# Latent attention, first head of a layer: the last memory head's transposes and values, and the pair's projection, placed inside the first gate chunk

## What is computed

```python
for l in range(DEPTH_2):                       # 2 layers
    h = rmsnorm_2(x, pre_norm_g[l])
    z = h @ w_in[l]
    q_lat, kv_lat, k_pe, gb, gc, xin, q_mem, gate = split_cols(z)
    q = (rmsnorm_2(q_lat, q_norm_g[l]) @ w_uq[l])       # 8 heads, 128 + 64 rotated columns
    kv = (rmsnorm_2(kv_lat, kv_norm_g[l]) @ w_ukv[l])   # 8 heads, 128 of key, 128 of value
    a_out = mla_attention(q, k, v)                      # the latent attention
    c_out = short_gated_conv(gb, gc, xin, conv_w[l])
    m_out = memory_attention(q_mem, mem_n, w_mk[l], w_mv[l])   # 4 heads over 256 memory tokens
    y = jnp.concatenate([a_out, c_out, m_out], axis=-1) * jax.nn.silu(gate)
    x = x + rmsnorm_2(y @ w_o[l], post_norm_g[l])
```

## Time and profile before

| what | value |
|---|---|
| median of 3 runs | 2345.44 us |
| lowest, highest run | 2343.36, 2347.05 us |
| the profiled execution | 2344.45 us |
| its span in the trace | 2342.6 us |
| PE busy | 2277.9 us (97%) |
| PE weight loads busy | 1863.3 us (80%) |
| DVE busy | 1186.3 us (51%) |
| ACT busy | 798.8 us (34%) |
| POOL busy | 184.2 us (8%) |
| mean granted clock of the PE | 0.993 |

### The profile page before, as it was taken

One profiled execution on the slowest core, in us unless ns is written; L12 is line 12 of the kernel. 1 busy time (PEld: TensorE's weight loads), 2 busy tenths in 40 slices (PEclk: granted clock), 3 DMA queues, 4 the chain that ended last, 5 costly groups with the idle time before them and its releaser, 6 DMA issues.

```text
span 2342.6 us, 28762 instructions
## 1 busy us (share of the span) xinstructions
PE 2277.9 (97%) x10726; PEld 1863.3 (80%) x10726; DVE 1186.3 (51%) x1531; ACT 798.8 (34%) x1216; POOL 184.2 (8%) x172
## 2 busy tenths in 40 slices
PE   7999999999999999999999999999999999999995
PEld 6888888878888888878877788878888787877884
DVE  7666666772238543445455532475433544554124
ACT  5443434352335411332333322344113323333220
POOL 4111111101110100000000011101000000000113
PEclk9999999999999999999999999999999999999997
DMA  7321222223237232212221222462322221213221
GB/s 282 113 72 72 72 83 78 76 98 114 90 142 263 81 108 90 70 61 78 75 87 57 113 91 106 150 246 72 108 90 72 75 79 59 87 66 138 107 90 72
DMA packets 36648, 238.98 MB, mean 102 GB/s; under 512 B 4192, under 2 KB 4448, under 8 KB 12896
## 3 DMA queue, kind: packets, MB, share of 16 engines
q1 hardware_dynamic: 29808, 204.47, 24.2%
q10 hardware_dynamic: 6336, 25.17, 2.8%
q0 software_dynamic: 432, 8.39, 0.9%
HBM read 221.24 MB, written 16.78 MB: 102 GB/s over the span
## 4 chain that ended last, share of the span: by engine, by line
PE 85%; DVE 7%; ACT 4%; issue 2%; DMA 1%; ACTq 0%; SPq 0%; POOL 0%; DVEq 0%; POOLq 0%
PE acc L415 68%; PE sc L415 4%; PE ov L721 2%; PE ov L415 2%; PE sc L710 1%; ACT hi L758 1%; ACT prob L1043 1%; PE ov L549 1%; PE sc L537 1%; DMA raw<-w_dram 1%; DVE lo L1082 1%; PE acc L429 1%; PE acc L430 1%; PE acc L433 1%; DVE st L1521 1%
## 5 line engine op out<-in xcount | busy, mean ns | idle before, releaser
L415 PE MATMUL acc<-h_hi,hi 128*128 128x512 f32 x2480 | 985.3, 397 | 27.3 <-DVE h_lo L1144 15.0
L415 PE MATMUL acc<-h_lo,hi 128*128 128x512 f32 x2480 | 967.8, 390 | 0.0
L415 PE MATMUL acc<-h_hi,lo 128*128 128x512 f32 x2480 | 967.5, 390 | 0.0
L1082 DVE TENSOR_TENSOR lo<-raw,hi 128x2048 fp32r<-128x2048 f32 (+2 forms) x196 | 432.7, 2208 | 492.1 <-ACT hi L758 489.8
L415 PEld LDWEIGHTS acc<-h_hi,hi 128*128 128x128 f32 x2480 | 467.1, 188 | 135.5 <-issue 28.8
L415 PEld LDWEIGHTS acc<-h_lo,hi 128*128 128x128 f32 x2480 | 467.2, 188 | 98.7 <-issue 5.3
L415 PEld LDWEIGHTS acc<-h_hi,lo 128*128 128x128 f32 x2480 | 466.8, 188 | 98.2
L758 ACT ACTIVATE hi<-raw 128x2048 fp32r<-128x2048 f32 (+2 forms) x196 | 361.5, 1844 | 275.2 <-PE acc L415 225.5
L765 ACT ACTIVATE sq<-acc 128x512 f32<-128x512 f32 x48 | 28.7, 599 | 358.5 <-PE acc L415 334.7
L827 ACT ACTIVATE prob<-prob,st 128x256 f32<-128x256 f32 x128 | 63.3, 496 | 136.6 <-DVE st L1204 136.6
L321 POOL TENSOR_TENSOR sqacc<-sqacc,sq 128x512 f32<-128x512 f32 x42 | 54.6, 1300 | 402.4 <-ACT sq L765 402.4
(11 more groups left out here) (217 smaller groups left out, 2489.3 us busy)
## 6 DMA issues: line engine op xcount, KB each, us to landing
raw<-w_dram SPq DMA_DIRECT2D x172, 1024.0 KB, 4.7
xr<-residual ACTq DMA_DIRECT2D x16, 512.0 KB, 5.7
residual<-g ACTq DMA_DIRECT2D x16, 512.0 KB, 4.2
raw<-w_dram SPq DMA_DIRECT2D x8, 896.0 KB, 4.4
raw<-w_dram SPq DMA_DIRECT2D x8, 768.0 KB, 5.4
g<-xT_dram SPq DMA_DIRECT2D x4, 1024.0 KB, 11.3
residual<-g POOLq DMA_DIRECT2D x1, 4096.0 KB, 13.8
area<-memT_dram POOLq DMA_DIRECT2D x2, 2048.0 KB, 9.2
```

The lines of the kernel that those rows point to most:

```text
L415: ins = pe.matmul(to, a, b, start=first and n == 0, stop=last and n == 2)
L1082: dve.tensor_tensor(lo[c.slot][:, 0:width], raw[c.slot][:, 0:width], hi[c.slot][:, 0:width].bitcast(F32), ALU.subtract).then_inc(lo_done, 1)
```

## The change

Only the order on the PE changes. The first head's projection stops behind the 18 matmuls into `acc` and `ov[1]`, and `features(ga)` begins. In front of its k-tile 2 stand the 8 transposes of the last memory head, and in front of its k-tile 6 the wait for `ptm_done`, `values_mem(3)` and the projection of the pair, whose last matmul now counts `chunk_done` of hc. The remaining 10 k-tiles of ga follow, and count `chunk_done` of ga. All other heads keep their order.

```diff
-                def project(c, j, free_banks):
+                def product(c, to, at, x, first, last, w_moves=False):
+                    w = slice(at, at + (2 * P if w_moves else P))
+                    return passes(to, hi[c.slot][:, w], lo[c.slot][:, w], m_hi[:, x], m_lo[:, x], first, last, w_moves)
+
+                def project(c, j):
 
                     begin(c)
...
-                    if j == 0:
-                        free_banks()
-                        for k in range(QRT):
-                            product(bank(0), k * QW[j] + P, tile(KVRT + k), k == 0, k == QRT - 1)
-                        for b in range(TB):
-                            for k in range(KVRT):
-                                ins = product(bank(1 + b // 2, 2 * P, b % 2 * 2 * P), UV + k * 2 * P,
-                                              slice(k * S + b * P, k * S + (b + 1) * P), k == 0, k == KVRT - 1, True)
-                    ins.then_inc(chunk_done, 1)
+                    return ins
+
+                def project_pair(c):
+
+
+                    for k in range(QRT):
+                        product(c, bank(0), k * QW[0] + P, tile(KVRT + k), k == 0, k == QRT - 1)
+                    for b in range(TB):
+                        for k in range(KVRT):
+                            ins = product(c, bank(1 + b // 2, 2 * P, b % 2 * 2 * P), UV + k * 2 * P,
+                                          slice(k * S + b * P, k * S + (b + 1) * P), k == 0, k == KVRT - 1, True)
+                    return ins
...
-                def end_of_memory():
-                    turn_mem(MH - 1)
-                    pe.wait_ge(ptm_done, l * MH + MH)
-
                 def head(i, j, first=False):
 
                     no = l * MLA + (i * 2 + (j + 1))
-                    project(chunk2(l, HEAD + 3 * j, i, 6), j, end_of_memory if first else lambda: turned_read(no - 1))
-                    if first:
+                    hc = chunk2(l, HEAD + 3 * j, i, 6)
+
+                    def end_of_memory():
+                        pe.wait_ge(ptm_done, l * MH + MH)
                         values_mem(MH - 1)
-                    else:
+                        project_pair(hc).then_inc(chunk_done, 1)
+
+                    ins = project(hc, j)
+                    if j == 0 and not first:
+                        turned_read(no - 1)
+                        ins = project_pair(hc)
+                    if not first:
+                        ins.then_inc(chunk_done, 1)
                         values_head(no - 1, 1 - j)
-                    features(chunk2(l, HEAD + 3 * j + 1, i, 6), h_hi, h_lo)
+                    features(chunk2(l, HEAD + 3 * j + 1, i, 6), h_hi, h_lo,
+                             meanwhile=[(2, lambda: turn_mem(MH - 1)), (6, end_of_memory)] if first else [])
```

More of the change, by code:

```diff
@@ L670, in _ @@
                     scores_mem(c)
-                def project(c, j, free_banks):
+                def product(c, to, at, x, first, last, w_moves=False):
+                    w = slice(at, at + (2 * P if w_moves else P))
+                    return passes(to, hi[c.slot][:, w], lo[c.slot][:, w], m_hi[:, x], m_lo[:, x], first, last, w_moves)
+                def project(c, j):
                     begin(c)
[L675 to L679, removed]
                     for k in range(QRT):
-                        product(acc[c.slot][:, :], k * QW[j], tile(KVRT + k), k == 0, k == QRT - 1)
+                        product(c, acc[c.slot][:, :], k * QW[j], tile(KVRT + k), k == 0, k == QRT - 1)
                     for k in range(KVRT):
-                        ins = product(ov[1][:, :], UK[j] + k * P, tile(k), k == 0, k == KVRT - 1)
-                    if j == 0:
-                        free_banks()
-                        for k in range(QRT):
-                            product(bank(0), k * QW[j] + P, tile(KVRT + k), k == 0, k == QRT - 1)
-                        for b in range(TB):
-                            for k in range(KVRT):
-                                ins = product(bank(1 + b // 2, 2 * P, b % 2 * 2 * P), UV + k * 2 * P,
-                                              slice(k * S + b * P, k * S + (b + 1) * P), k == 0, k == KVRT - 1, True)
-                    ins.then_inc(chunk_done, 1)
+                        ins = product(c, ov[1][:, :], UK[j] + k * P, tile(k), k == 0, k == KVRT - 1)
+                    return ins
[7 more added lines that the diff above has]
+                    return ins
                 def scores_head(no, i, j):
```

## The result

| | median us (lowest to highest, runs) | ratio to the kernel before, 95% interval |
|---|---|---|
| before | 2344.93 (2343.36 to 2347.05, 6) | |
| with the change | 2356.97 (2354.84 to 2358.87, 6) | 1.0049 (1.0039 to 1.0059) |

The change costs 12.0 us by the medians, and by the ratio 11.5 us (9.1 to 13.8). The profiled execution of the changed kernel took 2354.84 us with a span of 2353.0 us. It lies at the low end of its runs, 10.4 us over the profiled execution before.

The account below looks back on a forecast made before the run. The PE, busy 97% of the span, was taken to bound the kernel. 2 x (0.52 + 0.87 + 0.23 + 2.48) = 8.20 us plus 3.90 for the clock, on 2345.44, gave 2357.5 us, range 2351.0 to 2362.0.

Parts of the forecast that it names:

- later start behind the wait for ga: Behind the first head's projection: PE waits 4.0 us for DVE's split of ga and starts 0.52 us later per layer.
- transposes on the path: The 8 memory transposes, before done inside the waiting, now stand on the path between k-tiles of ga: +0.87 us per layer.
- scores wait for qk_done: Before the first head's scores: only 30 matmuls of ga follow the pair's projection, so scores wait +0.23 us per layer.
- 16 transposes behind the pair's end: First head's 16 transposes start at C + 22.24, held by the softmax in DVE's order: +2.48 us per layer.
- C: The end of the pair's projection in the first latent head, from which the forecast counts later steps in us.
- clock behind the wait for ga: Behind the 4.0 us wait the clock falls to 0.50, costing 2.74 us in each layer; range ends 0 and 2.74.
- clock behind the wait for the softmax: Behind the 2.48 us wait in gb the clock stays at 2.4 GHz: 0, upper end 1.58 to 2.74 us.
- (b): Rival: the clock falls in the softmax wait too, adding 1.58 to 5.48 us, 2359.1 to 2363.0 us; chance 0.18.
- (a): Rival: the clock stays up behind the long wait in one layer or both, 2354.8 or 2352.1 us; chance 0.22.
- (c): Rival: no wait for the softmax, DVE running its products ahead; 2352.6 us, or 2347.1 with full clock; chance 0.07.
- (e): Rival: the change does not reach the PE as written; 2345.4 us; chance 0.03.
- (d): Rival: ga is ready when the projection ends, both old waits go, 1.4 us faster, 2344.0 us; chance 0.05.

Follow-up runs that it names:

- ga early: Changed kernel with the split of ga moved ahead: on ACT before the last memory head's exponentials, on DVE behind that softmax's shift; ratio 0.9995 to the kernel before.
- both moves: Changed kernel with ga's split made early and, second, the first latent head's softmax ahead of its competitors on ACT and DVE; ratio 0.9967 to the kernel before.
- the control: Kernel before with the early split of ga alone, the PE's order unchanged; ratio 1.0002 to the kernel before.
- the last kernel but one: Kernel before, PE order unchanged, with the softmax ahead of the split of the next chunk in all 16 heads; ratio 0.9971 to the kernel before.
- the second of them in all heads: Changed kernel with ga's split early and the softmax ahead of the next chunk's split in all 16 heads; 2332.78 us, ratio 0.9950 to the kernel before.
- the filled wait: Changed kernel with the first head's key projection made three times, leaving 1.1 us of the 3.84 us wait idle; ratio 1.0035 to the kernel before.

## Why the prediction was right

The predicted 2357.5 us lies 0.5 us from the measured median; the range held it, and the sign was right. The mechanism was right too: the split of ga as the new wait, the transposes on the path, and the softmax late by DVE's order. That the median came within 0.5 us is luck, since the profile rose by 10.4 us and not by 12.1, and the clock's terms were not as forecast. The steps one by one, per layer:

| step | forecast us | profile us |
|---|---|---|
| later start behind the wait for ga | +0.52 | +0.34, +0.35 |
| transposes on the path | +0.87 | +1.51, +1.14 at the low clock (what exceeds 0.87 is also in the clock's row); +0.87 where it was high (ga early, both moves) |
| scores wait for qk_done | +0.23 | +0.23, +0.23 |
| 16 transposes behind the pair's end | C + 22.24 | C + 22.05, C + 22.04 |
| clock behind the wait for ga | +2.74 | +1.57, +1.49; in other kernels up to 2.79 |
| clock behind the wait for the softmax | 0 | 0, +1.6 |

*The wait for ga.* The forecast said 4.0 us and the trace says 3.84. The difference is the 0.23 us behind a split, taken from another place. Here it was 0.04 us. Ga early against the changed kernel shows that nothing else held the PE.

*The transposes* and *the scores* are as forecast. *The softmax* was forecast from DVE's own order, step by step, and came within 0.2 us. The path to the transposes grew by 2.5 us: 22.05 us where 25.34 - 5.81 = 19.53 us would have stood. Of this 0.23 us are the scores' wait, and 2.29 us the softmax's, for which 2.48 us were forecast; the idle time reads 2.01 us. Besides, the 16 transposes themselves take 1.97 us behind the wait and not 1.75, 0.22 us that the forecast left out. From the scores of the memory head to the end of these transposes, with the clock's falls taken off, the changed order costs 4.07 us per layer by the traces, beside the forecast's 0.52 + 0.87 + 0.23 + 2.48 = 4.10.

*The clock* is where two terms were missized, in opposite directions. The price of the fall behind ga was taken from one row at 1547 us. In the profiled execution it was 1.5 us in both layers, and over six cases 2.1 us on average. The fall behind the softmax wait was priced at nothing, by the row with 2.42 us, and rival (b) had it with 0.18. In this execution it came in the second layer, where the 16 transposes and the 24 matmuls behind them took 2.51 + 6.54 us and not 1.97 + 5.46:

```profile
1868.51 2.51 PE sc L711 x16
1871.02 6.54 PE acc L415 x24
```

And the kernel before pays for a fall more often than its one trace showed. The first head keeps that order in the control and in the last kernel but one, and the clock fell there in both layers of both, for 1.4 to 1.6 us, so in five of six stretches with the one before. With these averages, 2.1 us behind ga, 5/8 of 1.6 us behind the softmax and 2 x 5/6 of 1.5 us in the old order, the sum is 2 x (4.07 + 2.1 + 1.0) - 2.5 = 11.8 us, beside the measured 11.5. This is an estimate from six to eight cases each. The forecast's 3.90 us for the clock was a fair size for the wrong split: in the profile it is 1.57 + 1.49 + 1.62 - 1.58 = 3.10 us, by the averages 3.7 us. That the parts make up for each other was luck.

*The profile's difference* of 10.4 us is 3.84 + 5.34 us from scores to transposes, 1.6 us of clock behind them in the second layer, 2 x 0.22 us for the transposes behind a wait, and -0.8 us elsewhere: +2.0 us ahead of the first stretch and -2.9 us between the two, where both kernels do the same. The clock's falls near 730, 1550 and 2310 us come and go between executions of these kernels.

*The rivals.* (a), (c) and (e) did not come: the clock did not stay up behind ga, the softmax did wait, and the order was as written. (b) came in one of the two layers. (d) is what the early split then made of it: with ga ready in time there was no change to be told (0.9995), by the mechanism that (d) named and near the 2344 us that (d) gave. That the number agrees is partly luck, since (d) had nothing for the clock behind the softmax wait, which fell there in both layers of the trace, for 1.7 us each.

## What to carry to other kernels

Before a product is moved up into a wait, ask when its own operands are ready: work that hid behind the wait (here the split of ga, 3.8 us late) becomes the new wait. A block moved ahead of its consumer's other work also takes away the cover of whatever hangs on it (here DVE's and ACT's 22 us chain to the softmax), so recount every such chain from the moved block's end. Waits that the change creates can be cheap to cure by the order on the engines that wait for nothing: the two moves made of +0.5% a kernel 0.3% faster than before, and 0.5% with the second of them in all heads. But try each move in the old order too: there the second one alone, in all heads, gave 0.3%.

## What the runs showed of the hardware

A wait of the PE costs more than its idle time: 2.01 us of idle time in front of the 16 transposes stood for 2.29 us on the path to them and 0.22 us within them, and to that comes the clock. Behind waits of 3.84 us the granted clock fell to its lower level in six of six cases, for 1.4 to 2.8 us more time. Behind 1.10 and 1.30 us with 1.09 us of transposes between, it fell in five of six cases of the old order, for 1.4 to 1.6 us, and behind 1.10 and 1.64 us with the transposes between in two of two. Behind 2.0 us it fell in five of eight, and behind 1.12 us (the filled wait) and 1.40 us in none of two each. The same wait in the same kernel can have it in one layer and not in the other, which fits the 3 to 9 us by which runs of one kernel differ. With 24 matmuls, whose result was there already, put into the two waits of 3.84 us, the clock stayed up in both layers, and the kernel came out 3.3 us faster by the ratios, with every run under those without them.
